# Cache pages over half of the partitions, in rows of two successive keys

## The chip, the cores and the metric

The kernel runs on one core of a Trainium2 chip. The metric is the device time of one execution in microseconds (us), the median over runs. The core has five engines that run side by side, each with its own order of instructions: TensorE (PE, matmuls), VectorE (DVE), ScalarE (ACT), GpSimd (POOL, which here issues DMAs) and SyncE (SP, which only issues DMAs). Sixteen DMA engines move the data between HBM and SBUF, the on-chip memory of 128 partitions. Matmuls write to PSUM, in banks of 128 partitions by 512 columns.

## The reference, cut to what matters

One layer of a decoder trunk is computed for a prompt of 512 tokens and for a group of eight samples with one new token each. The change touches the attention of the eight samples over their cached keys and values. Each sample has 4096 past keys in 32 pages of 128 keys; a key or value is 8 heads by 64 numbers in float32, 2 KB. The pages of a sample lie anywhere in a pool, and `page_table` names them.

```
z       = q . k / sqrt(d) + bias                      # per sample, head and key
log_keep = log_sigmoid(-z)
later   = reverse cumsum(log_keep) - log_keep         # over the keys behind this one
w       = exp(log_sigmoid(z) + later)
y       = sum over keys of w * v
```

The rest of the layer (prompt attention, gated linear attention, a projection, the product-key experts with 16 of 16,384 experts for each of 8 heads and token, and an embedding gate) is the same in both kernels.

## The kernel before

**Two stages.** The front stage has the projections, both attentions and the gates of the first prompt half; the pages of the sample group are loaded and used in it. Behind it come the experts: GpSimd gathers 520 times 128 rows of 8 KB (L814), VectorE makes dot products (L1792), ScalarE weights (L1269 to L1280) and TensorE sums (L2425). The first gather waits on GpSimd until the folded values of all eight samples are done (`v_done`) and ScalarE has copied them (`y_taken`). The first prompt half's remaining weights and the second half's layer run beside the experts.

**Keys.** GpSimd loads key pages in quads of four (L761) into `kring`, a ring of three quads. A page is one DMA of 128 rows of 2 KB: key p of the page goes to partition p, and the page has one slot of 512 columns. VectorE multiplies a quad by the sample's query, copied to all partitions (L1367), and sums it by head (L1372), which frees the quad (`k_sum`). These steps, `keys(n)`, stand by hand between VectorE's other work: normalizations, masks and states of the two attentions that TensorE and ScalarE wait for. The scores lie in `zs` as partition = key in page, column = sample, head, page.

**Sum over later keys.** For two samples at a time (512 columns, q = 0 to 3) VectorE makes softplus values `part_l` and a running sum of them over the pages of a row, `part_sum` (`scores_softplus`; `page_reset` starts each row anew). TensorE sums over partitions in `later_keys`: a triangular matrix times `part_l` for the keys of the same page (L2017), and a matrix of -1 times the running sum of the page before (L2018).

**Values.** Value pages go to `vring`, a ring of eight slots. SP loads the first 160, those of five samples (L587, `early_pages`), in its one queue among the weights (L557, three slots of 512 KB) and small transfers; GpSimd loads the last 96 behind the keys, into both rings. Each page is one matmul with eight columns of weights (`v_page`, L2028), which frees the slot (`v_free`, `v_wide_free`). TensorE's order is written by hand: halves of eight pages' rings (`v_half`, four pages) stand between projections, heads of the prompt attention and gates. A page of the first five samples has its own semaphore; the others share one for four pages.

**Other narrow transfers.** Three transfers that the change leaves alone play a part below. `other_rows` (L632) copies token rows of 4 KB within SBUF, from partitions 0 to 63 to 64 to 127 and the other way, two DMAs a call:

```
def other_rows(t):
    for to, of in both_halves:
        sp.dma_start(xsw[to, t % 2], xn2row(t)[of]).then_inc(xsw_landed[t % 2], 16)
```

`other_lists` (L640, L641) does the same with short rows. And at L736 SP loads eight times one 4 KB row from HBM into 16 partitions, a different 16 each time.

Of the kernel before, what the change touches and what calls it, by code (L numbers as in the profile page):

```python
# [19 lines left out]
P = 128  # L20
# [11 lines left out]
H = 8  # L32
# [121 lines left out]

CONSTS = {}


def _consts():
# [9 lines left out]
        ("page_reset", np.broadcast_to(np.arange(512) % PAGES != 0, (P, 512))),  # L168
# [58 lines left out]
def build(nc, A):  # L227
    with ExitStack() as ctx:
# [83 lines left out]
        part_l, part_sum = view("part")[:, 0:512], view("part")[:, 512:1024]  # L312
# [225 lines left out]

        def value_slot(n):

            if n < V_FIRST:
                return vring[:, n % RING_V], v_early[n % RING_V], 16 * (n // RING_V + 1)
            i, s = divmod(n - V_FIRST, RING_K + RING_V)
            slot = kring[:, s] if s < RING_K else vring[:, s - RING_K]
            return slot, v_wide[s // HALF_V], 16 * HALF_V * (i + 1)
# [6 lines left out]
        def _(sp):  # L552
# [28 lines left out]
            def early_pages(first, end):  # L581
                for n in range(first, end):
                    if n % RING_V == 0:
                        read_numbers[n // RING_V] = page_numbers(mybir.EngineType.SP, n, RING_V)
                    page, s = read_numbers[n // RING_V][n % RING_V], n % RING_V
                    sp.wait_ge(v_free, n + 1)
                    sp.dma_start(vring[:, s, :], A["cache_v"][bass.ds(page, 1)].rearrange("a p n -> (a p) n")).then_inc(v_early[s], 16)  # L587
# [162 lines left out]
        def _(pool):  # L750
# [9 lines left out]
            def load_page(slot, cache, landed, page):  # L760
                pool.dma_start(slot, cache[bass.ds(page, 1)].rearrange("a p n -> (a p) n")).then_inc(landed, 16)  # L761

            for n in range(NB * PAGES // QUAD):
                if n % 2 == 0:
                    pages = page_numbers(mybir.EngineType.Pool, n * QUAD, 2 * QUAD)
                i = n % K_QUADS
                pool.wait_ge(k_sum, n + 1)
                for u in range(QUAD):
                    load_page(kring[:, QUAD * i + u], A["cache_k"], k_landed[i], pages[QUAD * (n % 2) + QUAD - 1 - u])
            following = page_numbers(mybir.EngineType.Pool, V_FIRST, RING_V)  # L770
            for i in range(V_FIRST // RING_V, NB * PAGES // RING_V):
# [3 lines left out]
                for s in range(RING_V):  # L775
                    n = i * RING_V + s
                    slot, landed, _ = value_slot(n)
                    if n < V_FIRST + RING_K:
                        pool.wait_ge(k_sum, K_QUADS + NB * PAGES // QUAD)
                    elif n < V_FIRST + RING_K + RING_V:  # L780
                        pool.wait_ge(v_free, RING_V + n - RING_K - RING_V + 1)
                    else:
                        pool.wait_ge(v_wide_free, n - V_FIRST - RING_K - RING_V + 1)
                    load_page(slot, A["cache_v"], landed, pages[s])
# [538 lines left out]
        def _(dve):  # L1323
# [72 lines left out]
            def scores_softplus(q):  # L1396
                dve.wait_ge(dec_l, q + 1)
                c.also(V.scalar_tensor_tensor, out=part_l, in0=two_samples(q), scalar=0.0, in1=part_l, op0=ALU.max, op1=ALU.add)
                c.then(V.tensor_tensor_scan, part_sum, cst("page_reset"), part_l, 0.0, ALU.mult, ALU.add, signal=dec_sp)
# [460 lines left out]
        def _(pe):  # L1860
# [151 lines left out]
            def later_keys(q):  # L2012

                pe.wait_ge(dec_sp, q + 1)
                late = lambda x: x.rearrange("p (r g) -> p r g", g=PAGES)
                out = bank[KEYS_BANK[q]][:, :]
                mm(out, cst("neg_tri"), part_l, start=True, stop=True)  # L2017
                mm(late(out)[:, :, 1:PAGES], wide("neg_one"), late(part_sum)[:, :, 0:PAGES - 1],  # L2018
# [5 lines left out]
            def v_page(b, n, group):  # L2024
                slot, landed, count = value_slot(b * PAGES + n)
                pe.wait_ge(landed, count)
                at = PAGE_COLS * group
                mm(bank[V_BANK[b]][at:at + H, :], w4[:, b, PAGES - 1 - n], slot, start=False, stop=True,  # L2028
# [564 lines left out]
```

## Time and profile before

| | |
|---|---|
| median of 3 runs | 2034.21 us (2033.65 to 2038.71) |
| profiled execution | 2041.42 us, its span 2039.7 us |
| TensorE matmul / VectorE / ScalarE / GpSimd busy | 76% / 67% / 33% / 38% of the span |
| DMA | 769.77 MB, mean 377 GB/s |
| granted TensorE clock, mean | 0.885 of full speed |

Busy shares are shares of the span. The DMA share of a window is the mean busy share of the 16 DMA engines in it; as it is summed from packets by their start, it can come out a little over 1. A page of 256 KB is 262,144 bytes. The DMA packets in the profile are pieces of 4096 bytes for GpSimd's pages and of 2048 for SP's.

### The profile page before, as it was taken

Reading aid. Unit: us, or ns where it says so; the run is one execution under the profiler, and the core shown is the slowest. Engines: PE = TensorE matmul, PEld = TensorE weight load, DVE = VectorE, ACT = ScalarE, POOL = GpSimd, SP = SyncE. Lnnn points to the kernel's source line nnn. Section 1 sums busy time; section 2 is a strip of 40 time slices with the busy share of each in tenths; the row PEclk is TensorE's granted clock in tenths of the full one; section 3 lists DMA queues with packets and bytes.
Section 4 is the critical chain, followed back from the end, with each engine's and each line's share of the span. In section 5 each row is a group of like instructions: output and inputs, shape, how many; then the busy total and the mean of one; then the engine's idle time right before and its main releaser. Section 6 shows DMA issues by size and latency. Waiting matters only on the chain. (4 is left out here: it accounts for less than half of the span.)

```text
span 2039.7 us, 24294 instructions
## 1 busy us (share of the span) xinstructions
PE 1551.8 (76%) x8264; PEld 732.3 (36%) x8264; DVE 1366.5 (67%) x2607; ACT 669.1 (33%) x1859; POOL 778.0 (38%) x882
## 2 busy tenths in 40 slices
PE   8999889999987776876786767676457558576656
PEld 6737535575464333433321323332112112122112
DVE  5988797792177786556645567877577787455544
ACT  3222145411123444344323223333233423223224
POOL 2432232233614433434343444444234344334441
PEclk9999899999998999889898889888678779678778
DMA  7877998999989999999999999999999999999996
GB/s 245 273 266 252 348 329 309 339 334 355 361 347 368 418 420 417 418 415 418 414 416 420 397 420 418 417 399 421 416 389 407 405 417 403 389 411 413 422 421 249
DMA packets 157996, 769.77 MB, mean 377 GB/s; under 512 B 26880, under 2 KB 27416, under 8 KB 90416
## 3 DMA queue, kind: packets, MB, share of 16 engines
q0 software_dynamic: 103072, 637.59, 77.9%
q1 hardware_dynamic: 54800, 130.63, 17.6%
q8 instruction: 65, 1.06, 0.2%
q14 instruction: 59, 0.48, 0.1%
HBM read 759.93 MB, written 5.56 MB: 375 GB/s over the span
## 5 line engine op out<-in xcount | busy, mean ns | idle before, releaser
L2425 PE MATMUL bank<-arena 64*64 64x512 f32 x4096 | 636.4, 752 | 427.1 <-ACT arena L1280 421.7
L1792 DVE CUSTOM_DVE_ANT_0 arena<-arena 128x1024 f32<-128x1024 f32 x520 | 630.4, 1227 | 459.2 <-DMA arena<-experts_in,arena 451.2
L814 POOL DMA_INDIRECT arena<-experts_in,arena x520 | 586.9, 1129 | 854.1 <-PE bank L2425 743.9
L2425 PEld LDWEIGHTS bank<-arena 64*64 64x64 f32 x4096 | 159.2, 159 | 850.8 <-ACT arena L1280 617.0
L1269 ACT ACTIVATE arena<-arena 128x2 f32<-128x2 f32 x260 | 52.8, 203 | 881.0 <-DVE arena L1792 873.0
L761 POOL DMA_DIRECT2D arena<-cache_k_in x256 | 137.8, 538 | 310.6 <-DVE arena L1372 270.3
L1280 ACT ACTIVATE arena<-arena 128x64 f32<-128x64 f32 (+1 forms) x520 | 152.3, 340 | 8.5
L1367 DVE TENSOR_TENSOR arena<-arena 128x2048 f32<-128x2048 f32 x64 | 146.1, 2283 | 6.2 <-ACT arena L206 5.1
L1372 DVE TENSOR_REDUCE arena<-arena 128x32 f32<-128x2048 f32 x64 | 146.3, 2287 | 1.9
L206 DVE TENSOR_TENSOR arena<-arena 128x512 f32<-128x512 f32 (+9 forms) x215 | 130.1, 610 | 20.8 <-DMA arena<-xT_in 8.5
L206 ACT ACTIVATE arena<-bank 128x512 f32<-128x512 f32 (+7 forms) x127 | 53.4, 438 | 250.6 <-PE bank L1896 88.6
L2337 PE MATMUL bank<-arena 128*128 128x256 f32 (+1 forms) x512 | 128.4, 405 | 7.1 <-DVE arena L206 5.1
L2268 PE MATMUL bank<-arena 128*128 128x256 f32 (+1 forms) x512 | 122.9, 395 | 8.3 <-DVE arena L206 7.1
L1274 ACT ACTIVATE arena<-arena 128x1 f32<-128x1 f32 x520 | 124.7, 287 | 8.5
L206 ACT ACTIVATE arena<-bank,arena 128x512 f32<-128x512 f32 (+4 forms) x144 | 76.5, 556 | 139.7 <-PE bank L2268 77.9
L2337 PEld LDWEIGHTS bank<-arena 128*128 128x128 f32 x512 | 99.9, 200 | 47.2 <-issue 24.0
L2268 PEld LDWEIGHTS bank<-arena 128*128 128x128 f32 x512 | 97.7, 195 | 44.5 <-issue 17.5
L2028 PE MATMUL bank<-arena 128*8 128x512 f32 x512 | 96.6, 608 | 13.6 <-DMA arena<-cache_v_in 13.6
L1896 PE MATMUL bank<-arena 128*128 128x260 f32 (+1 forms) x448 | 103.8, 385 | 3.8 <-DVE arena L206 2.4
L206 DVE TENSOR_TENSOR arena<-arena,bank 128x512 f32<-128x512 f32 (+3 forms) x76 | 39.6, 553 | 83.9 <-PE bank L2292 33.6
L1896 PEld LDWEIGHTS bank<-arena 128*128 128x128 f32 x448 | 83.1, 189 | 23.1 <-issue 6.5
L206 ACT ACTIVATE arena<-arena 128x260 f32<-128x260 f32 (+11 forms) x125 | 73.5, 596 | 47.1 <-DVE arena L206 20.3
(130 smaller groups left out, 1367.8 us busy)
## 6 DMA issues: line engine op xcount, KB each, us to landing
arena<-cache_k_in POOLq DMA_DIRECT2D x256, 256.0 KB, 5.2
arena<-w_stream_in SPq DMA_DIRECT2D x125, 512.0 KB, 11.6
arena<-cache_v_in SPq DMA_DIRECT2D x160, 256.0 KB, 6.6
arena<-cache_v_in POOLq DMA_DIRECT2D x96, 256.0 KB, 6.6
arena<-experts_in,arena POOLq DMA_INDIRECT x520
arena<-xT_in SPq DMA_DIRECT2D x4, 520.0 KB, 6.6
arena<-x_rows_in SPq DMA_DIRECT2D x2, 1024.0 KB
arena<-arena SPq DMA_DIRECT2D x8, 256.0 KB, 12.1
```

Of the source, the lines that this page charges most:

```text
L206: op(*args, **kw).then_inc(sem, 1)
L761: pool.dma_start(slot, cache[bass.ds(page, 1)].rearrange("a p n -> (a p) n")).then_inc(landed, 16)
L814: pool.indirect_dma_start(gring[:, s, :], None, A["experts"], bass.IndirectOffsetOnAxis(ap=rows, axis=0)).then_inc(g_landed[s], 16)
L1274: last = A_(coef[:, s:s + 1], weight, ACT.Copy, scale=act_g[:, s:s + 1])
L1280: last = A_(rows, mask, ACT.Copy, scale=coef[:, s:s + 1])
L1367: V.tensor_tensor(four, four, qbc[:, b:b + 1, :].to_broadcast([P, QUAD, PAGE_ROW]), ALU.mult).then_inc(k_mul, 1)
L1372: V.tensor_reduce(z4[:, b:b + 1, first:first + QUAD, :].rearrange("p a c h -> p (a c) h"), kring[:, QUAD * i:QUAD * i + QUAD].rearrange("p ...
L1792: last = V.tensor_tensor_reduce(gring[:, s, 0:D], gring[:, s, 0:D], x_rows, 1.0, 0.0, ALU.mult, ALU.add, dot[:, s:s + 1])
L1896: last = mm(out, w[:, k], xn[:, k, a:b], start=(k == 0), stop=(k == KD - 1))
L2268: last = mm(bank[4 + u][:, 0:b - a], w[:, k], xn[:, k, a:b], start=(k == 0), stop=(k == KD - 1))
L2337: last = mm(bank[4 + j % 2][:, 0:b - a], w[:, k], xn2T[p][:, k, 0:b - a], start=(k == 0), stop=(k == KD - 1))
L2425: last = mm(bank[2 * r + c2][out, :], diag[rows, s], gring[rows, s, cols], start=start, stop=True, skip_group_check=True)
```

## The change

Two successive pages of a sample, n even and n + 1, now share two ring slots. The first lies in partitions 0 to 63 of both slots, the second in 64 to 127. A page's keys 2q and 2q + 1 follow one another in one partition's row of 4 KB. So each page is one DMA of 64 rows of 4 KB with half of the partitions as its destination, where it was 128 rows of 2 KB over all of them. The bytes, the number of DMAs, of quads and of value matmuls stay the same. A load into either slot of a pair waits until both slots are free (`n | 1`), and the first value matmul of a pair in the first five samples waits for both pages.

In the scores, a column now holds either the even or the odd keys of a pair of pages. The sum over later keys follows: VectorE adds the columns of a pair into `part_pair` (256 columns) and runs the sum of pages over these; TensorE multiplies the triangular matrix by the pair sums, each used for two columns, adds the even key's own value back to the odd column with an identity, and subtracts the pairs before.

```diff
--- before.py
+++ after.py
@@ -152,6 +152,10 @@
     return pass_use(p) + 32 + j
 
 
+PAIR_COLS = 2 * H * PAGES // 2
+PAIR_ROWS = (slice(0, HP), slice(HP, P))
+
+
 CONSTS = {}
 
 
@@ -165,7 +169,7 @@
         ("neg_mask", NEG * (i >= j)),
         ("keep_mask", i < j),
         ("gla_mask", (i <= j) & (i // CHUNK == j // CHUNK)),
-        ("page_reset", np.broadcast_to(np.arange(512) % PAGES != 0, (P, 512))),
+        ("page_reset", np.broadcast_to(np.arange(PAIR_COLS) % (PAGES // 2) != 0, (P, PAIR_COLS))),
         ("ident64", i % HP == j[:, 0:HP]),
         ("iota16", np.broadcast_to(np.arange(TOPK), (P, TOPK))),
         ("sample_of", np.arange(P)[:, None] // (P // NB) == np.arange(NB)[None, :]),
@@ -309,7 +313,7 @@
         xT = view("xT").rearrange("p (m t) -> p m t", m=8)
         qbc = view("xT")[:, 0:NB * PAGE_ROW].rearrange("p (b c) -> p b c", b=NB)
         zs = view("zs")
-        part_l, part_sum = view("part")[:, 0:512], view("part")[:, 512:1024]
+        part_l, part_sum, part_pair = view("part")[:, 0:512], view("part")[:, 512:512 + PAIR_COLS], view("part")[:, 512 + PAIR_COLS:1024]
         kring = view("kring").rearrange("p (s c) -> p s c", s=RING_K)
         vring = view("vring").rearrange("p (s c) -> p s c", s=RING_V)
         qa_sq = view("vring")[:, 0:2 * T].rearrange("p (u t) -> p u t", u=2)
@@ -536,13 +540,17 @@
 
             return bank[i % 6] if i < LATE_ITEM else bank[4 + i % 2]
 
+        def two_keys(cache, page):
+
+            return cache[bass.ds(page, 1)].rearrange("a (q u) n -> (a q) u n", u=2)
+
         def value_slot(n):
 
             if n < V_FIRST:
-                return vring[:, n % RING_V], v_early[n % RING_V], 16 * (n // RING_V + 1)
+                return vring, n % RING_V, v_early[n % RING_V], 16 * (n // RING_V + 1)
             i, s = divmod(n - V_FIRST, RING_K + RING_V)
-            slot = kring[:, s] if s < RING_K else vring[:, s - RING_K]
-            return slot, v_wide[s // HALF_V], 16 * HALF_V * (i + 1)
+            ring, slot = (kring, s) if s < RING_K else (vring, s - RING_K)
+            return ring, slot, v_wide[s // HALF_V], 16 * HALF_V * (i + 1)
 
         block = ctx.enter_context(nc.Block())
 
@@ -583,8 +591,8 @@
                     if n % RING_V == 0:
                         read_numbers[n // RING_V] = page_numbers(mybir.EngineType.SP, n, RING_V)
                     page, s = read_numbers[n // RING_V][n % RING_V], n % RING_V
-                    sp.wait_ge(v_free, n + 1)
-                    sp.dma_start(vring[:, s, :], A["cache_v"][bass.ds(page, 1)].rearrange("a p n -> (a p) n")).then_inc(v_early[s], 16)
+                    sp.wait_ge(v_free, (n | 1) + 1)
+                    sp.dma_start(vring[PAIR_ROWS[s % 2], s - s % 2:s - s % 2 + 2], two_keys(A["cache_v"], page)).then_inc(v_early[s], 16)
 
             early_pages(0, RING_V)
             stream(16, 21)
@@ -757,8 +765,8 @@
             pool.dma_start(page_table[0:1, :], A["page_table"]).then_inc(table_landed, 16)
             pool.wait_ge(table_landed, 16)
 
-            def load_page(slot, cache, landed, page):
-                pool.dma_start(slot, cache[bass.ds(page, 1)].rearrange("a p n -> (a p) n")).then_inc(landed, 16)
+            def load_page(ring, first, half, cache, landed, page):
+                pool.dma_start(ring[PAIR_ROWS[half], first:first + 2], two_keys(cache, page)).then_inc(landed, 16)
 
             for n in range(NB * PAGES // QUAD):
                 if n % 2 == 0:
@@ -766,7 +774,7 @@
                 i = n % K_QUADS
                 pool.wait_ge(k_sum, n + 1)
                 for u in range(QUAD):
-                    load_page(kring[:, QUAD * i + u], A["cache_k"], k_landed[i], pages[QUAD * (n % 2) + QUAD - 1 - u])
+                    load_page(kring, QUAD * i + QUAD - 2 - (u - u % 2), u % 2, A["cache_k"], k_landed[i], pages[QUAD * (n % 2) + u])
             following = page_numbers(mybir.EngineType.Pool, V_FIRST, RING_V)
             for i in range(V_FIRST // RING_V, NB * PAGES // RING_V):
                 pages = following
@@ -774,14 +782,14 @@
                     following = page_numbers(mybir.EngineType.Pool, (i + 1) * RING_V, RING_V)
                 for s in range(RING_V):
                     n = i * RING_V + s
-                    slot, landed, _ = value_slot(n)
+                    ring, slot, landed, _ = value_slot(n)
                     if n < V_FIRST + RING_K:
                         pool.wait_ge(k_sum, K_QUADS + NB * PAGES // QUAD)
                     elif n < V_FIRST + RING_K + RING_V:
-                        pool.wait_ge(v_free, RING_V + n - RING_K - RING_V + 1)
+                        pool.wait_ge(v_free, RING_V + (n | 1) - RING_K - RING_V + 1)
                     else:
-                        pool.wait_ge(v_wide_free, n - V_FIRST - RING_K - RING_V + 1)
-                    load_page(slot, A["cache_v"], landed, pages[s])
+                        pool.wait_ge(v_wide_free, (n | 1) - V_FIRST - RING_K - RING_V + 1)
+                    load_page(ring, slot - slot % 2, slot % 2, A["cache_v"], landed, pages[s])
 
             pool.wait_ge(v_done, NB)
             pool.wait_ge(y_taken, 5)
@@ -1396,7 +1404,9 @@
             def scores_softplus(q):
                 dve.wait_ge(dec_l, q + 1)
                 c.also(V.scalar_tensor_tensor, out=part_l, in0=two_samples(q), scalar=0.0, in1=part_l, op0=ALU.max, op1=ALU.add)
-                c.then(V.tensor_tensor_scan, part_sum, cst("page_reset"), part_l, 0.0, ALU.mult, ALU.add, signal=dec_sp)
+                of_key = part_l.rearrange("p (g u) -> p u g", u=2)
+                c.then(V.tensor_tensor, part_pair, of_key[:, 0], of_key[:, 1], ALU.add)
+                c.then(V.tensor_tensor_scan, part_sum, cst("page_reset"), part_pair, 0.0, ALU.mult, ALU.add, signal=dec_sp)
 
             def scores_argument(q):
                 dve.wait_ge(dec_z, q + 1)
@@ -2012,20 +2022,26 @@
             def later_keys(q):
 
                 pe.wait_ge(dec_sp, q + 1)
-                late = lambda x: x.rearrange("p (r g) -> p r g", g=PAGES)
-                out = bank[KEYS_BANK[q]][:, :]
-                mm(out, cst("neg_tri"), part_l, start=True, stop=True)
-                mm(late(out)[:, :, 1:PAGES], wide("neg_one"), late(part_sum)[:, :, 0:PAGES - 1],
+                out = bank[KEYS_BANK[q]]
+                of_key = lambda x: x.rearrange("p (g u) -> p g u", u=2)
+                mm(of_key(out), cst("neg_tri"), part_pair.rearrange("p (g o) -> p g o", o=1).to_broadcast([P, PAIR_COLS, 2]),
+                   start=True, stop=True)
+                mm(of_key(out)[:, :, 1], ident, of_key(part_l)[:, :, 0], start=False, stop=True, skip_group_check=True)
+                by_row = lambda x: x.rearrange("p (r g u) -> p r g u", r=2 * H, g=PAGES // 2)
+                before = part_sum.rearrange("p (r g o) -> p r g o", g=PAGES // 2, o=1).to_broadcast([P, 2 * H, PAGES // 2, 2])
+                mm(by_row(out)[:, :, 1:PAGES // 2], wide("neg_one"), before[:, :, 0:PAGES // 2 - 1],
                    start=False, stop=True, skip_group_check=True).then_inc(dec_z, 1)
 
             w4 = zs.rearrange("p (b h g) -> p b g h", b=NB, h=H)
             zrow = cst("zero").to_broadcast([P, 512])
 
             def v_page(b, n, group):
-                slot, landed, count = value_slot(b * PAGES + n)
+                ring, slot, landed, count = value_slot(b * PAGES + n)
                 pe.wait_ge(landed, count)
+                if b < V_EARLY and n % 2 == 0:
+                    pe.wait_ge(v_early[slot + 1], count)
                 at = PAGE_COLS * group
-                mm(bank[V_BANK[b]][at:at + H, :], w4[:, b, PAGES - 1 - n], slot, start=False, stop=True,
+                mm(bank[V_BANK[b]][at:at + H, :], w4[:, b, PAGES - 2 - (n - n % 2) + n % 2], ring[:, slot], start=False, stop=True,
                    skip_group_check=True).then_inc(v_free if b < V_EARLY else v_wide_free, 1)
 
             def v_half(b, half):
```

## Rows read from the trace of the kernel before

**Rows 1.** Windows: PE, PEld, DVE, ACT, POOL busy us (instructions), clock, DMA share, GB/s.
```profile
0.00:22.00 22.00, 14.37 (x47) 9.67 (x47) 8.31 (x13) 6.81 (x10) 1.70 (x10) 1.00 0.66 231
22.00:136.00 114.00, 114.00 (x556) 74.33 (x557) 100.77 (x58) 32.82 (x74) 45.24 (x84) 1.00 0.74 248
136.00:200.00 64.00, 61.88 (x371) 42.87 (x369) 51.66 (x46) 18.51 (x41) 19.38 (x36) 1.00 0.80 287
200.00:400.00 200.00, 181.58 (x886) 91.96 (x886) 157.30 (x141) 86.31 (x139) 55.95 (x104) 0.93 0.93 331
400.00:460.00 60.00, 59.03 (x276) 48.45 (x275) 53.09 (x38) 8.73 (x15) 17.23 (x32) 1.00 0.93 330
460.00:578.00 118.00, 110.45 (x548) 58.65 (x547) 34.67 (x100) 18.12 (x35) 51.66 (x96) 1.00 0.99 358
578.00:2040.00 1462.00, 1010.47 (x5592) 406.37 (x5588) 960.67 (x2214) 497.79 (x1545) 586.86 (x520) 0.85 0.99 403
```

**Rows 2.** Timeline of GpSimd: start us, us, instruction, idle before it.
```profile
581.49 1.01 POOL L814 DMA_INDIRECT arena<-experts_in,arena  x1 [16.18 <-ACT arena L206]
```

**Rows 3.** Idle time of TensorE before the value matmuls (L2028): us, times.
```profile
  DMA arena<-cache_v_in: 55.3, 58
```

**Rows 4.** Groups by line, 0 to 578 us: busy, mean ns | idle.
```profile
L761 POOL DMA_DIRECT2D arena<-cache_k_in x256 | 137.8, 538 | 310.6 <-DVE arena L1372 270.3 <-DVEq L1345 20.4 <-issue 11.3
...
L1372 DVE TENSOR_REDUCE arena<-arena 128x32 f32<-128x2048 f32 x64 | 146.3, 2287 | 1.9
L1367 DVE TENSOR_TENSOR arena<-arena 128x2048 f32<-128x2048 f32 x64 | 146.1, 2283 | 6.2 <-ACT arena L206 5.1 <-DMA arena<-cache_k_in 1.0
```

**Rows 5.** DMA issues of the page: count, KB each, us to landing.
```profile
arena<-cache_k_in POOLq DMA_DIRECT2D x256, 256.0 KB, 5.2
...
arena<-cache_v_in SPq DMA_DIRECT2D x160, 256.0 KB, 6.6
```

**Rows 6.** DMA queues, 200 to 400 us: packets, MB, share (q1 SP, q0 GpSimd).
```profile
q1 hardware_dynamic: 19593, 38.19, 54.1%
q0 software_dynamic: 8513, 27.89, 38.7%
```

**Rows 7.** Timeline of SP: start us, us, narrow copies and loads.
```profile
541.73 2.62 SPq L632 DMA_DIRECT2D arena<-arena  x4
...
1126.85 1.16 SPq L632 DMA_DIRECT2D arena<-arena  x2
...
1738.01 3.67 SPq L736 DMA_DIRECT2D arena<-scratch_x  x8
```

**Rows 8.** Two windows without narrow transfers, columns as in rows 1.
```profile
530.00:544.00 14.00, 10.96 (x66) 4.93 (x65) 4.28 (x6) 7.12 (x13) 8.61 (x16) 1.00 1.03 391
1700.00:1738.00 38.00, 26.99 (x136) 8.38 (x136) 28.57 (x41) 13.36 (x42) 19.17 (x17) 0.86 1.01 419
```

**Rows 9.** DMA queues, 546.5 to 554.5 us.
```profile
q0 software_dynamic: 302, 1.00, 52.6%
q1 hardware_dynamic: 299, 0.97, 50.4%
```

**Rows 10.** DMA queues, 1130 to 1138 us.
```profile
q0 software_dynamic: 275, 2.01, 79.5%
q1 hardware_dynamic: 178, 0.53, 21.6%
```

**Rows 11.** DMA queues, 1745 to 1755 us.
```profile
q0 software_dynamic: 296, 2.16, 82.8%
q1 hardware_dynamic: 298, 0.53, 21.2%
```

**Rows 12.** Groups of VectorE by line and form, 0 to 578 us.
```profile
L206 DVE TENSOR_TENSOR arena<-arena 128x256 f32<-128x256 f32 x17 | 7.3, 427 | 0.6
L206 DVE TENSOR_TENSOR_SCAN arena<-arena 128x512 f32<-128x512 f32 x6 | 7.2, 1220 | 0.2
```

**Rows 13.** Line L2017: ns min/median/max, first and last start us, form.
```profile
L2017 PE MATMUL bank<-arena x8: 590/592/697, 179.5 to 501.6; 128*128 128x512 f32 x8
```

## The prediction

> **What bounds the kernel now.** I read the windows first, because the busy shares of the whole span mix two stages. From 578 us on, the core's DMA engines are full (share 0.99 at 403 GB/s [rows 1]), and the first gather of expert rows is issued at 581.49 us [rows 2]. So the second stage has 1458 us of transfers in front of it that the change doesn't touch, and the end moves by as much as that first gather moves. It waits for the folded values of all eight samples (`v_done`) and for ScalarE's copy of them, behind the last value page. The stage before is the one to look at.
>
> In that front stage TensorE is nearly always busy (110 to 114 us of each longer window, 181.58 of the 200 us from 200 to 400 [rows 1]). The value matmuls wait for DMA 58 times, 55.3 us in all [rows 3]. VectorE almost never waits for a key page (1.0 us [rows 4]); it is the loads that wait for VectorE (270.3 us, L761 [rows 4]). So transfers are a second limit close under TensorE. I multiply each window by its share and rate [rows 1]: the engines are occupied for 14.5 + 84.4 + 51.2 + 186.0 + 55.8 + 116.8 = 508.7 us of 578, and move 180.0 MB in them, 354 GB/s per occupied time. Of these bytes 134.2 MB are the 512 cache pages (256 key loads, 160 value loads of SP [rows 5], and the other 96 value loads; 262,144 bytes each). At 354 GB/s the pages take 379 of the 508.7 us. There are 69.3 us in which the engines are idle.
>
> **What the change does, part by part.**
>
> *Edits with one answer: page rows.* A page was 128 rows of 2 KB over all partitions; it becomes 64 rows of 4 KB over one half of them, and the next page goes to the other half. This alone saves little. From 200 to 400 us SP's queue, mostly 2 KB value rows, took 54.1% of 16 engines for 38.19 MB, and GpSimd's queue 38.7% for 27.89 MB [rows 6]: 45.3 against 44.4 engine-us per MB. If the 160 SP pages (41.9 MB) went at the second price, 41.9 x 0.9 / 16 = 2.4 us of occupied time would go.
>
> *The narrow destination.* This is the term that decides. No page goes to half of the partitions before, but three stretches hold narrow copies. `other_rows` (L632) copies 64 partitions of 4 KB each, two such copies a call, one into each half. At 541.73 us four of them are issued, at 1126.85 us two [rows 7]. The undisturbed rate is 391 GB/s just before the first and 419 in the gathers' stage [rows 8]. While they move, the DMA engines stay full (the two queues' shares sum to over 1), yet the rate falls: 1.97 MB in 8.0 us, 246 GB/s [rows 9], and 2.54 MB in 8.0 us, 317 GB/s [rows 10]. I take out GpSimd's bytes at the undisturbed rate and charge the rest to the copies. First: 8.0 us less 1.00 MB / 391 GB/s = 5.4 us for 0.97 MB, which is 14.8 packets of 4096 bytes for each of 16 engines, 368 ns a packet. Second: 8.0 less 2.01 MB / 419 = 3.2 us for 0.53 MB, 8.1 packets, 397 ns. A full-width packet of the same size costs 4096 x 16 / 391 = 168 ns. These copies read SBUF; one narrow transfer in the trace reads HBM as pages do: at 1738.01 us SP issues eight of 16 partitions each [rows 7]. From 1745 to 1755 us the rate is 269 GB/s against 419 [rows 8, 11], so 10.0 less 2.16 / 419 = 4.8 us go to 0.53 MB, 598 ns a packet. So one eighth of the partitions costs 3.6 times a full packet, and one half (read from SBUF) 2.2 to 2.4 times.
>
> For half a width read from HBM I take twice the best full-width packet, 2 x 4096 x 16 / 419 = 313 ns, below the copies, since a page isn't read from SBUF. The bounds are 168 ns (no effect) and 397 ns. The Trainium skill (SBUF — State Buffer, section on the DMA port swizzle) says that partitions 0 to 63 reach 8 of 16 ports, 218 GB/s at best and 196 measured; its next section, on two DMAs that hit both halves, has two concurrent ones only 6% over a single one. By 218 GB/s the pages would take 616 us, by 196 x 1.06 = 208 GB/s 645 us. The rows of this case agree with it as far as they go: neither pairs to opposite halves nor eight consecutive narrow transfers kept the rate.
>
> With 313 ns the 512 pages cost 512 x 4 = 2048 packets for each engine, 641 us in place of 379: +262 us. The occupied time of the front becomes 508.7 + 262 = 771 us. The idle time can't all be filled: 7.5 us lie ahead of 22 us, before the first key page, and both rings stay as short as they are (12 key pages, 8 value pages). With 7.5 to 69.3 us of idle left the front lasts 778 to 840 us against 578, +200 to +262. I take +231, the middle. With 397 ns it is 813 us for the pages, +434, less 0 to 62 of filled idle: +372 to +434; with 168 ns nothing.
>
> *Where the stall goes.* The key loads are the first to be late. A quad of four pages occupies the engines for 16 x 0.313 = 5.0 us alone, and twice that beside value pages; VectorE takes 2283 + 2287 ns for it [rows 4]. So VectorE, now waited for, will wait at L1367. Behind it in its order stand the normalizations and the masks that TensorE needs. The value matmuls wait longer on their side. Behind SP's page loads stand its weight loads in one queue, so that weights come late too, and every page reload of GpSimd waits for the matmul or the sum that frees it.
>
> *The pair's waits.* A value page of the first five samples now waits for both pages of its pair, and a reload waits until both were read (`n | 1`). The second matmul then finds its page. The delay is one page's time, 0.67 us at 391 GB/s, for 80 pairs at most: 0 to 54 us if nothing covers it, and it lies inside the +231, since the engines are then full. The wide pages waited for four already. GpSimd's issue is 538 ns a page [rows 4], 16 x 0.538 = 8.6 us per four quads against 18.3 us of VectorE; it stays covered, with 64 rows or with 128.
>
> *The sum over later keys.* Each of four calls gains one 128x256 addition on VectorE (427 ns for that shape) and its scan shrinks from 512 to 256 columns, from 1220 to some 610 ns: -0.7 us in all [rows 12]. TensorE gains a matmul of 256 columns, in two instructions like the others: 592 ns for 512 columns [rows 13], so 0.6 us a call, or 1.2 if the write at every second column costs double; with its weight load hidden, +2.4 to +4.8 us in four calls. The other matmul loses 16 of 496 columns. Under a front that waits for transfers this lies beside them; I count 0, and +2 to +5 us without that cover.
>
> **Sum.** The profiled execution took 2041.42 us (span 2039.7 and 1.7 around it); +231 gives 2272. The median of the runs is 2034.21, 7.2 lower, so I predict 2265 us.
>
> **Rivals.** (a) *The halves part.* Two successive pages go to opposite halves, and key and value queues mix. If some DMA engines run on one half while the others are on the other, the price lies between 168 and 313 ns, say 235: 2048 x 0.235 = 481 us, +102, less 0 to 62 of idle: +40 to +102, about 2105. Against it: the copies also alternated halves, among packets of another queue, and no relief shows in [rows 9, 10]. For it: the copies are at most four in a row. (b) *Loads from HBM don't mind.* Only copies that also read SBUF are slow. Then the price stays, the matmul and the pair's waits cost a little and the rows gain 2.4 us: 2034, within 5 either way. [rows 11] speaks against it. (c) *Faster.* As (b), but the longer rows bring value pages earlier. It decides where a page lands well under today's 6.6 us [rows 5]: a third less would take a third of the 55.3 us of waits, -18, 2016 us. Against it: the 2% in [rows 6].
>
> **How the numbers follow.** Main case 0.72, with its own range 2190 to 2430; (a) 0.17; (b) 0.05; (c) 0.06. A measurement of this kernel can tell some 0.3%, 6 us, from no change. Slower: 0.72 + 0.17 = 0.89; same 0.05; faster 0.06. The range runs from 2095, which leaves out the lower half of (a) (0.09) and (b) and (c) (0.11), to 2430, a little over the low end of the 397 ns case (2034 + 372 = 2406): 0.20 outside.
>
> **What the changed profile would show.** Right: the DMA share near 1 before the first gather, at 220 to 290 GB/s in place of 248 to 358; key and value pages landing after 9 us or more instead of 5.2 and 6.6; VectorE waiting for `cache_k_in` at L1367 for tens of us and TensorE for `cache_v_in` for more than 55.3; the first gather at some 810 us, and behind it a stage as long as before. The scan should take some 610 ns and the new matmul 300 to 600. Wrong would be a rate over 330 GB/s with the engines full. If rate and share both fall, rings and not width are the limit. If TensorE's granted clock falls with its idle time in the front (it is 0.93 from 200 to 400, where TensorE idles most, and 1.00 elsewhere [rows 1]), its own work grows and the time goes over 2265.

## The result, and the profile after

The change makes the kernel slower: 2192.59 us median (2177.27 to 2201.19) against 2035.56, a ratio of 1.0755 with a 95% interval of 1.0717 to 1.0794, +157 us. The forecast was 2265, +231. The profiled execution took 2177.27 us with a span of 2175.6, 135.9 over the one before. It was the fastest of the four, and the one profiled before (2041.42) was slower than the four runs of the kernel before, so the two traces show 136 of the 157 us.

The windows of the changed kernel, cut at the same times as [rows 1] where the stages allow it. Columns as there: TensorE, its weight loads, VectorE, ScalarE, GpSimd, granted clock, DMA share, GB/s.

```profile
0.00:22.00 22.00, 14.54 (x58) 10.05 (x62) 8.52 (x14) 7.08 (x11) 1.95 (x11) 1.00 0.63 225
22.00:136.00 114.00, 113.67 (x554) 73.73 (x546) 92.50 (x53) 32.66 (x74) 38.72 (x76) 1.00 0.98 238
136.00:200.00 64.00, 54.08 (x300) 37.52 (x299) 50.10 (x40) 14.04 (x31) 20.48 (x40) 0.89 0.99 261
200.00:400.00 200.00, 155.40 (x657) 75.66 (x655) 127.19 (x122) 60.68 (x104) 40.96 (x80) 0.75 1.01 250
400.00:460.00 60.00, 49.23 (x255) 23.63 (x256) 40.25 (x29) 26.48 (x40) 14.35 (x28) 0.91 1.01 252
460.00:600.00 140.00, 112.65 (x470) 79.38 (x464) 63.46 (x53) 16.33 (x27) 23.62 (x47) 0.90 1.01 252
600.00:714.00 114.00, 88.59 (x406) 40.85 (x406) 25.89 (x89) 14.62 (x30) 41.91 (x82) 0.90 1.01 270
714.00:2176.00 1462.00, 1004.66 (x5588) 403.64 (x5588) 960.19 (x2214) 497.62 (x1545) 595.01 (x520) 0.85 0.99 403
```

Read the last two columns downwards. From 22 us to the first gather the DMA engines are full, and they move 238 to 270 GB/s with it; before, they moved 248 to 358 at shares of 0.74 to 0.99. The last row has the length, the share and the rate of before (1462 us, 0.99, 403): the second stage has kept its length, and only its start moved. The timeline of GpSimd has that start:

```profile
716.69 1.02 POOL L822 DMA_INDIRECT arena<-experts_in,arena  x1 [16.03 <-ACT arena L210]
```

581.49 us before [rows 2], so +135.2 of the span's +135.9. A second trace of the changed kernel, that of the run `changed_again` below, has this gather at 731.77 us (+150.3) in a span of 2188.0 (+148.3); single traces of one kernel differ that much. The issues of the page (count, KB each, median us to landing) and two idle times, VectorE's before the key products (L1375, groups by line) and TensorE's before the value matmuls (L2044):

```profile
arena<-cache_k_in POOLq DMA_DIRECT2D x256, 256.0 KB, 9.0
...
arena<-cache_v_in SPq DMA_DIRECT2D x160, 256.0 KB, 12.0
arena<-cache_v_in POOLq DMA_DIRECT2D x96, 256.0 KB, 14.0
```

```profile
L1375 DVE TENSOR_TENSOR arena<-arena 128x2048 f32<-128x2048 f32 x64 | 146.4, 2287 | 67.3 <-DMA arena<-cache_k_in 62.1 <-ACT arena L210 5.1
```

```profile
  DMA arena<-cache_v_in: 122.4, 54
  issue: 110.2, 60
```

A key page lands after 9.0 us in place of 5.2, a value page of SP after 12.0 in place of 6.6 [rows 5]. VectorE, which waited 1.0 us for keys [rows 4], waits 62.1. TensorE's wait for value pages went from 55.3 us [rows 3] to 122.4. The 110.2 us of "issue" stand ahead of the same matmuls and were 20.6 before. The first matmul of a pair now waits for a second page, so some of it may be for DMA too; the profile doesn't say.

### The profile page after: what moved, and what is told of

It is laid out like the page before. It is cut to its first block, busy times and chain, and to the rows that moved or that the text cites. A ratio compares the mean times of both kernels' runs of the same rounds, so it can differ in the third digit from the quotient of the medians.

```text
span 2175.6 us, 24394 instructions
## 1 busy us (share of the span) xinstructions
PE 1592.8 (73%) x8272; PEld 744.5 (34%) x8272; DVE 1368.1 (63%) x2611; ACT 669.5 (31%) x1859; POOL 777.0 (36%) x882
## 4 chain that ended last, share of the span: by engine, by line
DMA 35%; PE 11%; DVE 8%; POOL 4%; issue 4%; ACT 3%; ACTq 0%; POOLq 0%; DVEq 0%
DMA arena<-experts_in,arena 35%; PE bank L2441 8%; POOL arena L822 4%; DVE arena L210 4%; DVE arena L1802 4%; PE bank L2419 2%; ACT arena L1288 1%; ACT arena L1282 1%; PE bank L2284 1%; ACT arena L1277 0%; PE bank L2353 0%; ACT arena L210 0%; PE bank L2472 0%; ACT L210 0%; ACT L1277 0%
## 5 line engine op out<-in xcount | busy, mean ns | idle before, releaser
L822 POOL DMA_INDIRECT arena<-experts_in,arena x520 | 595.0, 1144 | 847.6 <-PE bank L2441 726.9
L769 POOL DMA_DIRECT2D arena<-cache_k_in x256 | 131.1, 512 | 407.1 <-DVE arena L1380 351.4
L1375 DVE TENSOR_TENSOR arena<-arena 128x2048 f32<-128x2048 f32 x64 | 146.4, 2287 | 67.3 <-DMA arena<-cache_k_in 62.1
L2044 PE MATMUL bank<-arena 128*8 128x512 f32 x512 | 110.8, 700 | 88.3 <-DMA arena<-cache_v_in 88.3
L210 DVE TENSOR_TENSOR arena<-arena 128x512 f32<-128x512 f32 (+10 forms) x219 | 131.9, 607 | 26.7 <-ACT arena L210 12.5
L2284 PE MATMUL bank<-arena 128*128 128x256 f32 (+1 forms) x512 | 130.0, 411 | 12.7 <-DVE arena L210 6.7
L2353 PE MATMUL bank<-arena 128*128 128x256 f32 (+1 forms) x512 | 129.2, 407 | 8.8 <-DVE arena L210 5.5
L2284 PEld LDWEIGHTS bank<-arena 128*128 128x128 f32 x512 | 102.6, 205 | 55.2 <-issue 19.6
L2353 PEld LDWEIGHTS bank<-arena 128*128 128x128 f32 x512 | 100.5, 202 | 50.3 <-issue 25.0
L1906 PEld LDWEIGHTS bank<-arena 128*128 128x128 f32 x448 | 84.9, 193 | 27.5 <-issue 6.4
```

What stands on the lines that cost most here:

```text
L210: op(*args, **kw).then_inc(sem, 1)
L769: pool.dma_start(ring[PAIR_ROWS[half], first:first + 2], two_keys(cache, page)).then_inc(landed, 16)
L822: pool.indirect_dma_start(gring[:, s, :], None, A["experts"], bass.IndirectOffsetOnAxis(ap=rows, axis=0)).then_inc(g_landed[s], 16)
L1375: V.tensor_tensor(four, four, qbc[:, b:b + 1, :].to_broadcast([P, QUAD, PAGE_ROW]), ALU.mult).then_inc(k_mul, 1)
L1906: last = mm(out, w[:, k], xn[:, k, a:b], start=(k == 0), stop=(k == KD - 1))
L2284: last = mm(bank[4 + u][:, 0:b - a], w[:, k], xn[:, k, a:b], start=(k == 0), stop=(k == KD - 1))
```

## The experiments

**Transfers alone.** The disputed price was measured by itself: a kernel that has none of the layer and loads 48 cache pages at a time, one arrangement after another, each waited for, in one execution. The arrangements differ in the destination:

```
whole pages    e.dma_start(arena[:, 512 * n:512 * n + 512], page n as 128 rows of 2 KB)
wide           e.dma_start(slot(n // 2), pages n and n + 1 as 128 rows of 4 KB)
narrow         e.dma_start(slot(i)[rows], page n as 64 rows of 4 KB)
    rows       lower or upper half: in turns of 1, 2 or 4 pages, or the lower alone;
               or even and odd partitions in turns
```

> Leaves out the whole layer: it only loads 48 cache pages of 256 KB at a time, in one arrangement after another, each into its own place, and waits for all before the next arrangement. SP alone, then GpSimd alone, then both. Theory (width: two DMA engines share the way into a half, so a half-width packet costs up to twice a full one): pages over all partitions run near 390 to 420 GB/s, with 4 KB rows or 2 KB rows alike; pages that alternate between the halves, or go to the same half, run at 210 to 250 GB/s, with 2 KB or 4 KB rows; if the relief seen in the changed kernel (282 ns a packet where twice a full one is 313) comes from turns between the halves, the same half alone gives about 210 and turns of one page more. Rival 1 (row form: 64 rows of 4 KB are a bad form of DMA whatever their width): 4 KB rows over all partitions are slow too, 2 KB rows in halves are not. Rival 2 (only mixed queues or the kernel's waits make it slow): halves alone run above 350 GB/s. Every second partition in place of a half: near 400 if only the half matters, 210 to 250 if the number of partitions does.

Windows of that run, a us or two inside each arrangement; the last two columns are DMA share and GB/s.

```profile
2.00:35.00 33.00, 0.50 (x1) 1.00 1.03 379
38.00:69.00 31.00, 0.00 (x0) 1.00 0.99 395
72.00:126.00 54.00, 0.00 (x0) 1.00 1.03 231
129.00:188.00 59.00, 0.00 (x0) 1.00 1.03 209
191.00:250.00 59.00, 0.00 (x0) 1.00 1.03 212
253.00:286.00 33.00, 0.00 (x0) 1.00 0.99 381
289.00:341.00 52.00, 0.00 (x0) 1.00 1.07 237
344.00:401.00 57.00, 0.00 (x0) 1.00 1.03 219
...
737.00:793.00 56.00, 11.21 (x23) 1.00 1.03 224
796.00:840.00 44.00, 10.74 (x22) 1.00 1.04 282
```

In order, on SP's queue: whole pages 379 GB/s; wide 395; halves in turns of one 231; the lower half alone 209; turns of four 212; every second partition 381; halves with two rows of 2 KB 237; turns of two 219. The last two rows are both queues at once: each with turns of one 224, SP in the lower half with GpSimd in the upper 282. On GpSimd's queue alone the rates for whole, wide, turns, lower half and every second partition were 369, 390, 234, 210 and 386. So it is neither the row (4 KB rows are good when wide, 2 KB rows hardly better when narrow, 237 against 231) nor the number of partitions: 64 of them, taken every second, are within 4% of 128 with the same rows (381 against 395). It is that they are neighbours in one half; 64 neighbours across the middle, 32 to 95, were not tried. A page in turns of one costs 4096 x 16 / 231 = 284 ns a packet. The rival of bad row forms falls, and so does the one that only mixed queues or the kernel's waits make pages in halves slow.

The Trainium skill (SBUF — State Buffer, section "Can I just issue two DMAs to hit both halves?") says that only one transfer over all 128 partitions reaches all ports, and that two transfers to the two halves gain 6% over one. Here turns of one gain 231 / 209 = 11% and two queues with a half each 282 / 209 = 35%, and the every-second form contradicts the first. Its map of ports (section "Door 1: The DMA port swizzle") fits the measurement: by that map even partitions reach all of them.

**Everything but the narrow pages.** From the changed kernel, whole pages again:

```diff
-            return cache[bass.ds(page, 1)].rearrange("a (q u) n -> (a q) u n", u=2)
+            return cache[bass.ds(page, 1)].rearrange("a p n -> (a p) n")
-                pool.dma_start(ring[PAIR_ROWS[half], first:first + 2], two_keys(cache, page)).then_inc(landed, 16)
+                pool.dma_start(ring[:, first + half], two_keys(cache, page)).then_inc(landed, 16)
```

and the same on SP.

> The changed kernel with its waits for pairs and its sum over pairs of columns, but each page again as 128 rows of 2 KB over all partitions, one slot a page. The sum then pairs the wrong keys; the work is the same. Width theory: 2035 us, within 0.5% of the kernel before, since waits and sum lie beside other work (at most +5 us). Rival (the pair's waits or the longer sum cost the time): 2100 to 2190 us, a large part of the +157.

2043.70 us, a ratio of 1.0030 (1.0006 to 1.0055). The waits and the longer sum leave +6 us of the +157.

**The row alone.** The source becomes `"a (u q) n -> (a q) u n"`, two rows of 2 KB in each of 64 partitions.

> The changed kernel with pages in one half of the partitions, but in two rows of 2 KB for a partition in place of one of 4 KB (keys q and 64 + q of a page; the sum pairs the wrong keys). Width theory: 2180 to 2215 us, as the changed kernel or a little over it. Rival (the 4 KB row form costs the time): 2035 to 2080 us.

2216.74 us, 1.0865 (1.0812 to 1.0918). With 2 KB rows in halves the kernel is as slow as with 4 KB rows, and some 1% slower still. By the rate of such pages alone, 237 against 231 GB/s, it should not be. In the kernel the rate did fall: from 200 to 400 us, with shares of 1.00 and 1.01, its trace has 235 GB/s where the changed kernel's has 250. GpSimd's issue takes 587 ns a page there and 512 in the changed kernel. Which of these is the cause isn't shown.

**Wide rows of 4 KB.** Two pages of fixed place in one DMA over all partitions.

```diff
-            return cache[bass.ds(page, 1)].rearrange("a (q u) n -> (a q) u n", u=2)
+            return cache[page - page % 2:page - page % 2 + 2].rearrange("a (q u) n -> (a q) u n", u=2)
```

with one issue for each odd page, and half the count in the waits.

> The changed kernel with two pages in one DMA of 128 rows of 4 KB over all partitions, at fixed places of the pool in place of those of the page table (so other pages are read), half as many DMAs. Width theory: 2015 to 2040 us: rows of 4 KB over all partitions cost nothing, and may give back some of the 55 us that TensorE waits for value pages. Rival (row form): 2150 us or more.

2026.72 us, 0.9958 (0.9945 to 0.9971): the only variant faster than the kernel before. It can't be had with pages that lie anywhere in the pool, and it doesn't separate the rows of 4 KB from the halved number of DMAs.

**Every second partition.** What the run of loads alone pointed to, as a complete kernel:

```diff
-PAIR_ROWS = (slice(0, HP), slice(HP, P))
+PAIR_ROWS = (slice(0, P, 2), slice(1, P, 2))
+        ("neg_pairs", -1.0 * (i % 2 * HP + i // 2 >= j % 2 * HP + j // 2)),
-                mm(of_key(out), cst("neg_tri"), part_pair.rearrange("p (g o) -> p g o", o=1).to_broadcast([P, PAIR_COLS, 2]),
+                mm(of_key(out), cst("neg_pairs"), part_pair.rearrange("p (g o) -> p g o", o=1).to_broadcast([P, PAIR_COLS, 2]),
```

> The changed kernel with the first page of a pair on the even partitions and the second on the odd ones, still 64 rows of 4 KB each, and a triangular matrix in that order of partitions for the sum over later keys. In the run of loads alone such pages ran at 377 to 380 GB/s, pages in halves at 230, whole pages at 365 to 374. Theory (what costs is that 64 neighbouring partitions share half of the ways into SBUF): 2025 to 2045 us, like the version over all partitions. Rival (64 rows in a page, or the count of partitions, cost the time in the kernel, where two queues mix): 2100 us or more.

2037.75 us, 1.0016 (1.0003 to 1.0029). The two slices, with the matrix that follows them, take back all but 3 of the 157 us. Its DMAs have the same rows, sizes, waits and order as the changed kernel; only the partitions differ. Its landing times in the page are those of before or a little under:

```profile
arena<-cache_k_in POOLq DMA_DIRECT2D x256, 256.0 KB, 4.9
arena<-cache_v_in SPq DMA_DIRECT2D x160, 256.0 KB, 6.0
arena<-cache_v_in POOLq DMA_DIRECT2D x96, 256.0 KB, 5.9
```

It doesn't beat the kernel before. The next run bears on the 3 us that it is behind.

**The pair's waits alone**, on the kernel before:

```diff
-                    sp.wait_ge(v_free, n + 1)
+                    sp.wait_ge(v_free, (n | 1) + 1)
                 pe.wait_ge(landed, count)
+                if b < V_EARLY and n % 2 == 0:
+                    pe.wait_ge(v_early[(b * PAGES + n + 1) % RING_V], count)
```

and `n | 1` in GpSimd's two waits.

> The kernel before with one part of the change: a reload waits until both slots of its pair are read, and the first value matmul of a pair waits for both pages. Prediction: beside transfers that aren't full it can cost up to 54 us, and lies beside other work otherwise. If the +0.3% of the full-width version (2043.7 against 2035.6) comes from these waits: 2040 to 2045 us. If it comes from the longer sum over later keys: 2035 us.

2037.30 us, 1.0021 (1.0006 to 1.0037), +4 us. As far as the intervals tell, it can be all that the every-second version loses (+0.03 to +0.29%) and all or part of what the full-width version does (+0.06 to +0.55%). The longer sum's own share isn't settled: 2035 us were expected if it was to blame and 2040 to 2045 if the waits were, and the time fell between.

**Keys alone, values alone in halves.** Of the changed kernel one of the two kinds of pages is whole again. With narrow keys, for the value pages on GpSimd (the same on SP, and with narrow values for the key pages):

```diff
-                    load_page(ring, slot - slot % 2, slot % 2, A["cache_v"], landed, pages[s])
+                    pool.dma_start(ring[:, slot], whole_page(A["cache_v"], pages[s])).then_inc(landed, 16)
```

> The changed kernel with only the key pages in halves; value pages are whole again (so the two layouts disagree and the weights meet the wrong values; the work is the same). By the price of 282 ns for a half-width packet against 185 for a whole one, 1024 packets add 99 us of occupied time, and up to 62 us of idle time can be filled. Theory (idle time is filled first): +37 to +60 us, 2073 to 2095. Rival (each narrow page costs its full extra time): half of +157, 2113 us or more.

> The same with only the value pages in halves. The same sum of occupied time, +99 us, but values fall where the engines were fuller already (share 0.93 to 0.99 from 200 us on) and end the stage: theory +60 to +95 us, 2095 to 2130, more than with keys alone. Rival (keys are what VectorE waits for, so keys cost the time): values alone +0 to +40 us, less than keys alone.

2122.89 us, 1.0448 (1.0420 to 1.0477), and 2153.51 us, 1.0571 (1.0527 to 1.0615): +90 and +121. Both lie above what was expected, and together (211) above the 157 of the change itself. Values cost more than keys, as expected. The key version's time even falls where its rival, a narrow page costing its full extra time, had it (2113 or more), but not for that reason, as the windows show. Of the version with narrow keys, up to its first gather at 664.80 us:

```profile
22.00:136.00 114.00, 112.53 (x551) 73.49 (x548) 91.33 (x52) 32.73 (x74) 38.64 (x76) 1.00 0.99 234
136.00:200.00 64.00, 51.02 (x265) 34.78 (x264) 50.19 (x38) 11.75 (x25) 18.34 (x36) 0.89 1.02 259
200.00:400.00 200.00, 161.82 (x746) 82.15 (x744) 131.68 (x128) 69.56 (x120) 42.81 (x84) 0.80 0.97 264
400.00:460.00 60.00, 44.60 (x217) 20.18 (x216) 36.41 (x27) 22.29 (x35) 14.29 (x28) 0.85 1.03 266
```

With its other three windows (0.65 of the first 22 us, 0.97 of 460 to 575 and 0.96 of 575 to 664) they sum to 645 us of occupied time, +137 over the 508.7 of before for 1024 narrow packets, where 99 had been expected: 185 + 133 = 318 ns a packet, not 282, if the narrow packets are charged with all that is lost. The version with narrow values comes to 644 us in the same way, 317 ns. Idle time was filled where there was some: 19 of 69 us are left with narrow keys, so that its first gather came 83 us later and not 137. With narrow values 52 are left, since they are loaded from 136 us on and the 0.74 of 22 to 136 us stays:

```profile
22.00:136.00 114.00, 114.00 (x556) 74.38 (x556) 101.22 (x57) 32.79 (x74) 45.13 (x84) 1.00 0.74 251
```

So the form of the sum held and its price didn't: narrow and whole pages together cost more than the prices of each among its like add up to. The next run tests that by itself.

**Transfers alone, mixed.**

> Leaves out the layer: transfers alone again, each stage waited for. SP alone: 48 copies within SBUF between the halves (64 rows of 4 KB, as the copies on which the prediction sized the price), 24 copies over all partitions, 48 pages in alternating halves. Then both queues at once, 24 pages each: whole pages on SP with half-width pages on GpSimd; the other way round; both on every second partition; copies between halves on SP with whole pages on GpSimd. Theory (a half-width packet costs more among whole ones than among its like, since whole packets of the same DMA engine stand behind it and of another engine go to the same half): mixed pages run at 255 to 270 GB/s, where 285 would follow from 285 ns and 175 ns a packet; copies alone run at 230, like half-width loads, and among whole pages again cost 350 to 400 ns a packet. Rival (reading SBUF is what made the copies dearer): copies alone run at 180 GB/s or less, copies over all partitions well under 370, and the mixed pages at 285. Every second partition on both queues: 370 to 380.

The windows: copies within SBUF between halves; copies over all partitions; pages in halves; whole pages on SP with halves on GpSimd; the other way round; every second partition on both; copies between halves on SP with whole pages on GpSimd.

```profile
28.00:81.00 53.00, 0.00 (x0) 0.00 (x0) 1.00 1.03 234
84.00:114.00 30.00, 0.00 (x0) 0.00 (x0) 1.00 1.02 406
117.00:170.00 53.00, 0.00 (x0) 0.00 (x0) 1.00 1.03 234
172.00:221.00 49.00, 0.00 (x0) 12.14 (x24) 1.00 1.02 254
224.00:273.00 49.00, 0.00 (x0) 11.53 (x22) 1.00 1.02 255
276.00:307.00 31.00, 0.00 (x0) 10.62 (x21) 1.00 1.00 395
310.00:360.00 50.00, 0.00 (x0) 12.00 (x23) 1.00 1.03 251
```

The mixed pages run at 254 and 255 GB/s. 24 pages of each kind are 12.58 MB, 49.5 us at 254; the whole ones alone would take 6.29 MB / 379 = 16.6 us, so 32.9 us go to 96 narrow packets for each engine, 343 ns, if they are charged with all that is lost. Alone they cost 280 (234 GB/s). The copies read SBUF and are no dearer for it: 234 GB/s alone, and 251 among whole pages. The rival, that reading SBUF made the copies dear, falls.

The queues' own shares say which packets lost the time. From 174 to 214 us of this run, halves on GpSimd (q0) and whole pages on SP (q1); packets, MB, share of 16 engines:

```profile
q0 software_dynamic: 1875, 6.17, 63.4%
q1 hardware_dynamic: 1956, 3.58, 39.5%
```

That is 269 ns for a narrow packet (0.634 x 40 us for the 94 of each engine) and 289 ns for 4096 bytes of whole pages. By the same reckoning, with the shares a little over 1, turns of one alone took 294 ns, and whole pages on both queues 172 and 179 (run of loads alone, 74 to 124 and 702 to 734 us). With the queues exchanged, 226 to 266 us, it is 259 for narrow and 269 for whole. So the narrow packets cost no more among whole ones; it is the whole ones that slow down to their pace.

**The order of the halves.** In the changed kernel, `for u in (0, 2, 1, 3)` for the key pages of a quad, beside the changed kernel itself again.

> The changed kernel with the four key pages of a quad issued in the order first, third, second, fourth, so that two pages go to the same half before the other's turn. In the run of loads alone turns of two pages ran at 217 GB/s against 230 for turns of one (302 against 285 ns a packet). Theory (the turns between halves give the relief): 1024 key packets x 17 ns = +17 us over the changed kernel, 2200 to 2215 us. Rival (in the kernel two queues mix anyway, so the order within one doesn't matter): as the changed kernel, within 5 us.

> The changed kernel itself, on the same chip as the changed order of keys, to compare the two: 2180 to 2205 us, 1.070 to 1.082 times the kernel before.

2200.05 us, 1.0818 (1.0773 to 1.0862), against 2187.31 us, 1.0728 (1.0692 to 1.0764). The difference of 0.9% is 18 us by the ratios and 13 by the medians, with 17 expected. That the order costs something is only just shown: the two intervals part by 0.1%, and the changed kernel's first runs (1.0755, up to 1.0794) reach into that of the new order. The size agrees with what the run of loads alone had for turns of two; no more can be said.

## Why the prediction was right, and where its size was off

*What bounds the kernel.* Right. The second stage kept its length, and the first gather carried the whole loss (135.2 of 135.9 us). It came at 716.69 us, not at the 810 that was forecast.

*How near the miss was.* The direction and the mechanism were earned, the place in the range less so. The front's sum gave +200 to +262 at 313 ns, and the runs have +157. The 2192.59 us lie 2.6 above the low end of the main case's own range (2190), and the later set of runs of the same kernel (2187.31) below it. Rival (a) had +40 to +102, so the truth lies between the two cases, and two terms, the price of a packet and the idle time, missed in the same direction.

*The narrow destination.* The mechanism was right. It is shown by the every-second version, which differs from the changed kernel in which partitions a page goes to and in the matching matrix, and takes back all but 3 us. The price was too high. The changed kernel's windows sum to 13.9 + 111.7 + 63.4 + 202.0 + 60.6 + 141.4 + 115.1 = 708.1 us of occupied time, +199.4 in place of the forecast +262. That is (379 + 199.4) / 2048 = 282 ns a packet in place of 313. The second trace of the changed kernel, in the same way, has 724.1 us up to 728 us, 290 ns. 313 is nearly what one half alone costs (4096 x 16 / 209 = 314 ns); turns of one page cost 284 by themselves. So rival (a), that halves in turns give relief, was true with a small relief, 30 ns and not 78. The rows on which I leaned against it, [rows 9] and [rows 10], held copies among whole packets. I took out GpSimd's bytes at the undisturbed rate and so charged the copies with what the whole packets beside them had lost. That gave 368 and 397 ns, and the same reckoning gives 343 in the mixed run; it hid the relief. The copies' own shares in those rows, 50.4% of 8.0 us for 14.8 packets and 21.6% for 8.1, are 272 and 214 ns. In the changed kernel the whole transfers pay too. From 40 to 130 us SP's queue has no pages, mostly weights; before, and changed:

```profile
q1 hardware_dynamic: 1720, 6.00, 19.0%
```

```profile
q1 hardware_dynamic: 1727, 6.03, 26.5%
```

That is 187 ns for 4096 bytes before and 259 after, and the 282 ns above charge it to the pages. That copies read SBUF, my reason for going below their 368 to 397 ns, was the wrong reason: alone they cost what loads cost.

*The idle time.* The other term that was mis-sized. I left 7.5 to 69.3 us idle and took the middle; 708.1 of 714 us were occupied by the shares, so 6 us were left, at the low end. (A share of 1.01 counts more time than there is; with such shares taken as 1, 11 us were left, 8 of them ahead of 22 us.) The rings of 12 and 8 pages were long enough to keep full engines full. The two misses, 63 us of occupied time and 32 of filled idle time, make the 95 by which the profiled sum was too high. That +199.4 - 63 gives the profiled +136 is no check, since both come from the same windows.

*Where the stall goes.* As forecast: VectorE at L1375 with 62.1 us, and value pages with 122.4. TensorE's granted clock fell with it, to 0.75 from 200 to 400 us (0.93 before) and to 0.89 to 0.91 in the other windows from 136 us to the gather. The forecast took this as a way to end above 2265; with the engines full (0.99 to 1.01 in those windows) that slower work lay beside transfers.

*The pair's waits.* +4 us on the kernel before (1.0021), of the 0 to 54 that I had bounded. In the changed kernel they can't be told from the rest.

*The sum over later keys.* The scan of 256 columns took 692 ns, not 610, and the added matmul 388 ns in each of its two instructions, inside 300 to 600. The group by form on VectorE, the line on TensorE, and a group of other 256-column matmuls in the same trace, which write to successive columns:

```profile
L210 DVE TENSOR_TENSOR_SCAN arena<-arena 128x256 f32<-128x256 f32 x4 | 2.8, 692 | 0.1
```

```profile
L2029 PE MATMUL bank<-arena x8: 387/388/390, 192.7 to 613.0; 128*128 128x256 f32 x8
```

```profile
L1906 PE MATMUL bank<-arena 128*128 128x256 f32 x64 | 14.8, 383 | 0.0
```

8 x 388 ns = 3.1 us of TensorE's time in all. Writing to every second column cost next to nothing, 388 against 383. What the forecast had too cheap is the short matmul: at 256 columns it takes more than half of the 592 ns of 512. Whether any of the 3.1 us shows in the time isn't separated from the pair's waits.

*The row of 4 KB.* Small, as forecast from [rows 6]. Alone the wide form has 395 against 379 GB/s. In a kernel it is worth 0.4% together with half as many DMAs, and on every second partition nothing could be told, where the pair's waits stand against it.

What stays open: why two rows of 2 KB in a half cost the kernel 1% more than one of 4 KB, when alone their rate is no lower; and by what mechanism whole packets slow down beside narrow ones.

## What to carry to other kernels

Between 64 and 128 partitions a transfer's cost depended on which it reached, not on how many: 64 neighbours in one half ran at 55% (one half alone) to 61% (in turns) of the rate of 64 taken every second. Where data must go to a part of the partitions, spread them with a step and put the order into the constants of the matmul that follows. Look in the trace for any narrow transfer that is there already, at the bytes of both queues and at each queue's own share: what is lost in a mix may be lost by the transfers beside it. Such a window gives the price of a change before it is built, but only for the mix in which it ran. And when transfers become the limit of a stage that was nearly full before, count the idle time of the DMA engines as gone.

## What the runs showed of the hardware that I had not expected

Every second partition of 64 runs at 381 GB/s on SP's queue and 386 on GpSimd's, against 379 and 369 for whole pages in rows of 2 KB and 395 and 390 in rows of 4 KB. The length of the turns between halves matters: 231 GB/s for one page, 219 for two, 212 for four, 209 for one half alone. With each queue in its own half the rate is 282, the best of the forms in halves, yet far from 379. Whole pages beside narrow ones take 269 to 289 ns for 4096 bytes of their queue's own time, against 172 to 179 beside each other. Copies within SBUF over all partitions reach 406 GB/s, a little more than loads in the same rows of 4 KB at 395. A matmul that writes 256 columns with a step of two takes 388 ns against 383 without the step. SP's issue of a page went from 333 ns to 469 with 64 rows of 4 KB in a half, 475 on every second partition, and 599 with two rows of 2 KB a partition; GpSimd's from 538 to 512 and 587.
